# A two-layer encoder on one core: the first layer's entry with all its transfers on one queue, a split second piece and a turn between products

## The reference, cut to what matters

```
h    = rms_norm(x, ev_attn_norm)      # x / sqrt(mean(x*x) + eps) * gain, 256 x 1024
proj = h @ ev_w_in                    # 1024 x 2304
a_q, a_k, a_v, b_q, b_k, b_v = split(proj)
```

## Time and profile before

| | |
|---|---|
| median of 3 runs | 1421.13 us (1420.88 to 1421.44) |
| profiled execution | 1422.96 us, of which span of instructions 1420.8 us |
| PE busy | 1385.0 us, 97% of the span |
| DVE, ACT, POOL busy | 1162.4, 1043.4, 125.9 us |
| moved by DMA | 429.01 MB, mean 302 GB/s |

### The profile page before, as it was taken

One profiled execution on the slowest core, in us unless ns is written; L12 is line 12 of the kernel. 1 busy time (PEld: TensorE's weight loads), 2 busy tenths in 40 slices (PEclk: granted clock), 3 DMA queues, 4 the chain that ended last, 5 costly groups with the idle time before them and its releaser, 6 DMA issues.

```text
span 1420.8 us, 19392 instructions
## 1 busy us (share of the span) xinstructions
PE 1385.0 (97%) x6473; PEld 1133.6 (80%) x6473; DVE 1162.4 (82%) x1450; ACT 1043.4 (73%) x1351; POOL 125.9 (9%) x200
## 2 busy tenths in 40 slices
PE   7999999999899999999999999999999999999997
PEld 5866788888667888888888888888888888888885
DVE  4767555456896999898899989989989998998996
ACT  5566544446785878878878887887888888788786
POOL 0100000000620930000000000000000000000000
PEclk9989999999999999999999999999999999999999
DMA  9603954402807999999999999999999999999980
GB/s 342 257 0 111 363 180 140 144 23 75 326 18 296 371 381 385 376 372 391 363 388 384 369 385 380 380 374 370 393 363 389 388 372 385 370 385 371 373 331 15
DMA packets 132018, 429.01 MB, mean 302 GB/s; under 512 B 4177, under 2 KB 11516, under 8 KB 131980
## 3 DMA queue, kind: packets, MB, share of 16 engines
q1 hardware_dynamic: 126672, 416.82, 77.7%
q0 software_dynamic: 2480, 8.95, 2.5%
q10 hardware_dynamic: 2828, 2.75, 0.6%
HBM read 422.21 MB, written 6.29 MB: 302 GB/s over the span
## 4 chain that ended last, share of the span: by engine, by line
PE 86%; issue 6%; DVE 4%; ACT 2%; DMA 1%; POOL 0%; ACTq 0%; SPq 0%; DVEq 0%; POOLq 0%
PE bank L728 27%; PE bank L730 26%; PE bank L729 26%; PE bank L688 2%; PE bank L865 1%; ACT w_hi L1117 1%; DVE w_lo L1608 1%; DMA xres<-in_x_dram 1%; PE bank L850 0%; PE bank L857 0%; PE bank L849 0%; DMA out_dram<-h,idx_t 0%; PE bank L650 0%; PE bank L923 0%; ACT hT_hi L1145 0%
## 5 line engine op out<-in xcount | busy, mean ns | idle before, releaser
L1536 DVE TENSOR_TENSOR w_lo<-ring,w_hi 128x1024 fp32r<-128x1024 f32 x544 | 644.3, 1220 | 34.8 <-ACT w_hi L1053 20.6
L1053 ACT ACTIVATE w_hi<-ring 128x1024 fp32r<-128x1024 f32 x544 | 571.0, 1062 | 129.7 <-PE bank L730 129.7
L728 PE MATMUL bank<-w_hi,hT_hi 128*128 128x512 f32 (+3 forms) x1088 | 419.2, 385 | 2.4 <-DVE w_lo L1608 1.2
L730 PE MATMUL bank<-w_lo,hT_hi 128*128 128x512 f32 (+3 forms) x1088 | 417.1, 383 | 0.0
L729 PE MATMUL bank<-w_hi,hT_lo 128*128 128x512 f32 (+3 forms) x1088 | 416.9, 383 | 0.0
L728 PEld LDWEIGHTS bank<-w_hi,hT_hi 128*128 128x128 f32 x1088 | 205.1, 189 | 44.4 <-DVE w_lo L1608 3.1
L730 PEld LDWEIGHTS bank<-w_lo,hT_hi 128*128 128x128 f32 x1088 | 205.0, 188 | 40.0
L729 PEld LDWEIGHTS bank<-w_hi,hT_lo 128*128 128x128 f32 x1088 | 205.2, 189 | 39.1
L1608 DVE TENSOR_TENSOR w_lo<-ring,w_hi 128x1024 fp32r<-128x1024 f32 (+3 forms) x124 | 139.5, 1134 | 85.6 <-ACT w_hi L1117 85.4
L728 PE MATMUL bank<-w_hi,aT_hi 128*128 128x512 f32 x490 | 194.8, 398 | 3.4 <-issue 1.9
L730 PE MATMUL bank<-w_lo,aT_hi 128*128 128x512 f32 x490 | 191.6, 391 | 0.0
(11 more groups left out here) (326 smaller groups left out, 1189.7 us busy)
## 6 DMA issues: line engine op xcount, KB each, us to landing
ring<-in_od_e_gate_dram SPq DMA_DIRECT2D x57, 2048.0 KB, 9.5
ring<-in_od_e_up_dram SPq DMA_DIRECT2D x56, 2048.0 KB, 10.3
ring<-in_od_e_down_dram SPq DMA_DIRECT2D x56, 2048.0 KB, 10.1
ring<-in_ev_w_gate_dram SPq DMA_DIRECT2D x5, 2048.0 KB, 8.4
ring<-in_ev_w_up_dram SPq DMA_DIRECT2D x5, 2048.0 KB, 9.7
ring<-in_ev_w_down_dram SPq DMA_DIRECT2D x5, 2048.0 KB, 13.8
ring<-in_ev_w_in_dram SPq DMA_DIRECT2D x3, 2048.0 KB, 22.5
ring<-in_ev_w_out_dram SPq DMA_DIRECT2D x2, 2048.0 KB, 20.5
```

Source lines behind the costliest of these rows:

```text
L728: pe.matmul(dst, hi, whi, start=first, stop=False)
L730: return pe.matmul(dst, hi, wlo, start=False, stop=final)
L1053: act.activation(e_hi_at[place_of(q)], eights(ring[:, i % RING, j * QUARTER:(j + 1) * QUARTER]), ACT.Copy).then_inc(hi_ready, 1)
L1536: dve.tensor_tensor(e_lo_at[place_of(q)], eights(ring[:, i % RING, j * QUARTER:(j + 1) * QUARTER]), e_hi_at[place_of(q)].bitcast(F32), ALU ...
```

## The change

On SP the first constants transfer shrinks to the identity (128 columns instead of 384) and the rest moves behind piece 1. Piece 1 becomes four transfers with a semaphore each. The five transfers of `load_rows` leave ACT's queue for SP's: the bias ones behind piece 1, the sinks and gain rows behind piece 2. PE gets 14 matmuls of 128x128 float32 whose results nobody reads, and turns the second half of x between quarter 0 and quarter 1. ACT and DVE now take stripes 0 and 1 ahead of quarter 0 and stripes 2 and 3 ahead of quarter 1; ACT then does the sums of squares, then quarters 2 and 3, and both take stripes 4 to 7 last. DVE no longer waits for x at the start. The diff, blank lines left out:

```diff
--- before.py
+++ after.py
@@ -284,6 +284,7 @@
         arrived = [sem(f"arrived{i}") for i in range(RING)]
         first_arrived = [sem(f"first_arrived{j}") for j in range(4)]
+        second_arrived = [sem(f"second_arrived{j}") for j in range(3)]
         hi_ready = sem("hi_ready")
         lo_ready = sem("lo_ready")
         quarter_used = sem("quarter_used")
@@ -508,7 +509,19 @@
         @block.sync
         def _(sp):
-            sp.dma_start(cst[:, 0:C_DIST], const[:, 0:C_DIST]).then_inc(consts_loaded, 16)
+            def load_rows(which):
+                if which == "bias":
+                    for dst, keys in ((bias0, P), (bias1, 2 * P)):
+                        src = bass.AP(a["ev_b_rel_bias"].tensor, MAX_REL + 1 - P,
+                                      [[1, P], [2 * MAX_REL + 1, B_HEADS], [1, keys]])
+                        sp.dma_start(dst, src).then_inc(braw_loaded, 16)
+                else:
+                    sp.dma_start(sinks[:, :], a["ev_a_sinks"].to_broadcast([P, A_HEADS])).then_inc(rows_loaded, 16)
+                    sp.dma_start(gq[:, :], a["od_q_norm"].to_broadcast([P, C_QK])).then_inc(rows_loaded, 16)
+                    sp.dma_start(gk[:, :], a["od_k_norm"].to_broadcast([P, C_QK])).then_inc(rows_loaded, 16)
+            sp.dma_start(cst[:, 0:C_TRI], const[:, 0:C_TRI]).then_inc(consts_loaded, 16)
             for half in range(2):
                 cols = slice(half * NW, (half + 1) * NW)
                 sp.dma_start(xres[:, :, cols], x_in[0].rearrange("(t p) d -> p t d", p=P)[:, :, cols])\
@@ -518,8 +531,17 @@
                                  pieces[0]["src"][:, 2 * j:2 * j + 2, :]).then_inc(first_arrived[j], 16)
             for n, p in enumerate(pieces):
                 if n == 0:
-                    sp.dma_start(cst[:, C_DIST:], const[:, C_DIST:]).then_inc(tables_loaded, 16)
                     continue
+                if n == 1:
+                    for j in range(4):
+                        sp.dma_start(ring[:, 1, j * QUARTER:(j + 1) * QUARTER].rearrange("p (k n) -> p k n", k=2),
+                                     p["src"][:, 2 * j:2 * j + 2, :])\
+                          .then_inc(second_arrived[j] if j < 3 else arrived[p["place"]], 16)
+                    sp.dma_start(cst[:, C_TRI:], const[:, C_TRI:]).then_inc(tables_loaded, 16)
+                    load_rows("bias")
+                    continue
+                if n == 3:
+                    load_rows("gains")
                 before = [m for m in range(n) if pieces[m]["place"] == p["place"]]
                 if before:
                     sp.wait_ge(lo_ready, pieces[before[-1]]["q1"])
@@ -945,12 +967,23 @@
                         turn(c if p["kind"] == "up" else c + 1)
+            def idle_matmuls(n):
+                for _ in range(n):
+                    pe.matmul(bank[6][:, 0:P], ones[:, :], ones[:, :], start=True, stop=True)
+            pe.wait_ge(ones_set, 1)
+            idle_matmuls(5)
             pe.wait_ge(consts_loaded, 16)
             pe.wait_ge(gains_loaded, 16)
             pe.transpose(bank[7][:, 0:G_ALL], g_rows[:, :], ident[0:G_ALL, 0:G_ALL]).then_inc(gains_turned, 1)
-            turn_norm(0)
-            for q in range(IN_FIRST):
+            idle_matmuls(3)
+            turn_norm(0, (0, 1))
+            idle_matmuls(6)
+            in_quarter(0)
+            turn_norm(0, (2, 3))
+            for q in range(1, IN_FIRST):
                 in_quarter(q)
             heads0()
             turn_norm(1)
@@ -1108,6 +1141,10 @@
                     p = pieces[n]
                     if n == 0:
                         act.wait_ge(first_arrived[q], 16)
+                    elif n == 1 and q - p["q0"] < 3:
+                        act.wait_ge(second_arrived[q - p["q0"]], 16)
+                    elif n == 1:
+                        act.wait_ge(arrived[p["place"]], 16)
                     elif k0 == 0:
                         act.wait_ge(arrived[p["place"]], 16 * (p["turn"] + 1))
                     if q >= SPLITS:
@@ -1118,36 +1155,9 @@
                        .then_inc(hi_ready, 1)
                     split[0] += 1
-            def load_rows():
-                for dst, keys in ((bias0, P), (bias1, 2 * P)):
-                    src = bass.AP(a["ev_b_rel_bias"].tensor, MAX_REL + 1 - P,
-                                  [[1, P], [2 * MAX_REL + 1, B_HEADS], [1, keys]])
-                    act.dma_start(dst, src).then_inc(braw_loaded, 16)
-                act.dma_start(sinks[:, :], a["ev_a_sinks"].to_broadcast([P, A_HEADS])).then_inc(rows_loaded, 16)
-                act.dma_start(gq[:, :], a["od_q_norm"].to_broadcast([P, C_QK])).then_inc(rows_loaded, 16)
-                act.dma_start(gk[:, :], a["od_k_norm"].to_broadcast([P, C_QK])).then_inc(rows_loaded, 16)
-            def norm(n):
+            def square_sums(n):
                 if n == 0:
-                    act.dma_start(g_rows[:, :], a["gains"]).then_inc(gains_loaded, 16)
-                    act.wait_ge(eps_set, 1)
-                    act.activation(rt[:, 0:1], eps[:, 0:1], ACT.Sqrt)
-                    split_to(1)
-                    act.wait_ge(gain_cols_ready, 1)
-                for k in range(KD):
-                    if n == 0 and k % 2 == 0 and k:
-                        split_to(k // 2 + 1)
-                    if k % 2 == 0:
-                        act.wait_ge(hT_turned, 4 * n + k // 2 + 1)
-                    act.activation(hT_hi[:, k, :], bank[k // 2][:, (k % 2) * SEQ:(k % 2 + 1) * SEQ], ACT.Copy,
-                                   scale=g_cols[:, G_FWD[n] + k:G_FWD[n] + k + 1]).then_inc(hT_hi_ready, 1)
-                if n in SPLIT_FIRST:
-                    split_to(pieces[stage_pieces(SPLIT_FIRST[n])[0]]["q0"] + LEAD)
-                if n == 0:
-                    load_rows()
                     act.wait_ge(x_loaded[0], 16)
                     act.wait_ge(x_loaded[1], 16)
                     act.wait_ge(ones_set, 1)
@@ -1158,6 +1168,29 @@
                 link(sq)
                 act.activation(rt[:, NORM:NORM + TB], ss[:, NORM:NORM + TB], ACT.Sqrt, bias=eps[:, 0:1],
                                scale=1.0 / D).then_inc(norm_sqrt, 1)
+            def norm(n):
+                if n == 0:
+                    act.dma_start(g_rows[:, :], a["gains"]).then_inc(gains_loaded, 16)
+                    act.wait_ge(eps_set, 1)
+                    act.activation(rt[:, 0:1], eps[:, 0:1], ACT.Sqrt)
+                    act.wait_ge(gain_cols_ready, 1)
+                for k in range(KD):
+                    if n == 0 and k == 2:
+                        split_to(1)
+                    if n == 0 and k == 4:
+                        split_to(2)
+                        square_sums(n)
+                        split_to(4)
+                    if k % 2 == 0:
+                        act.wait_ge(hT_turned, 4 * n + k // 2 + 1)
+                    act.activation(hT_hi[:, k, :], bank[k // 2][:, (k % 2) * SEQ:(k % 2 + 1) * SEQ], ACT.Copy,
+                                   scale=g_cols[:, G_FWD[n] + k:G_FWD[n] + k + 1]).then_inc(hT_hi_ready, 1)
+                if n in SPLIT_FIRST:
+                    split_to(pieces[stage_pieces(SPLIT_FIRST[n])[0]]["q0"] + LEAD)
+                if n:
+                    square_sums(n)
             def projection(stage, then=None):
@@ -1881,8 +1915,6 @@
             dve.memset(eps[:, :], EPS).then_inc(eps_set, 1)
             dve.memset(ones[:, :], 1.0).then_inc(ones_set, 1)
-            dve.wait_ge(x_loaded[0], 16)
-            dve.wait_ge(x_loaded[1], 16)
             dve.wait_ge(consts_loaded, 16)
             norm(0)
```

## The result

The changed kernel takes **1416.06 us** in the median of 7 executions (1413.04 to 1417.96), the kernel before 1421.44 us (1418.16 to 1422.76) beside it: ratio 0.9965, 95% interval 0.9955 to 0.9975, so it is faster by about 5 us in 1421, which is small but clear of the interval. The forecast was 1415.8.

The account below looks back on a forecast made before the run. PE bounds the kernel, busy 1385.0 of 1420.8 us, and can still win at the entry: 2.7 + 2.9 + 1.25 - 1.0 - 0.55 = 5.3 us, so the median goes from 1421.13 to 1415.8, range 1413.8 to 1419.6.

Parts of the forecast that it names:

- the first product: On PE at the entry: the first product starts at 10.1 us instead of 12.80, 2.7 us won.
- the 48 products: Quarters 0 to 3 on PE: 48 products in 10.9 instead of 13.84 us at the higher clock, 2.9 us won.
- the wait of 1.25: PE before quarter 4: the wait while ACT issues transfers goes, 1.25 us won.
- the turns: PE between quarters 0 and 1: turning x's second half there costs 1.0 us.
- the new wait: PE before quarter 2: waits for stripes 4 and 5 behind sums of squares and both quarters, 0.55 us lost.
- The 5.3 us that I added to the first unread product: TensorE's clock at the entry: high from about 6.5 us, as 1.1 + 5.3 = 6.4.
- a clock that rises late: Rival at the entry: clock high only at about 13 us, 3.4 us gained, 1417.7; chance 0.15.
- Piece 2: Weights transfer for quarter 8: lands at 29.6 us, 1.6 us before ACT must start at about 31.2.
- the rival: Piece 2 lands 3.6 us later and PE waits 2 us at quarter 8: 1417.8; chance 0.10.
- The heads: Rival in the heads around 80 us: the low-clock stretch falls otherwise, 3 us of either sign, 1419; chance 0.07.
- Slower, at 1427.6: PE between 8.5 and 34 us: unread products don't raise the clock and delay real ones, 6.5 us lost; chance 0.07.

Follow-up runs that it names:

- the kernel with six in the heads: The changed kernel with six more unread products in the heads, four before the sixth head's scores and two before the seventh's: 1413.65 us, ratio 0.9952.

## Why the prediction was right, point by point

**Term by term.** Between the two profiles the first product is 2.3 us earlier (2.7 forecast), the 48 products take 11.4 us instead of 13.84 (2.4 won, 2.9 forecast), the wait of 1.25 is gone, the turns cost 0.8 (1.0) and the new wait 0.37 (0.55): 4.8 us at quarter 4 against the forecast 5.3. The way is the forecast one; that the median, 1416.06, came within 0.3 us of 1415.8 is in part luck, as a median of seven here depends on how many executions kept the clock in the heads.

**The first product**, forecast 10.1, came at 10.49, and for the named reason: with DVE's wait put back it is at 13.85. Two errors of mine nearly cancelled. I had the clock high from 6.5 us, but the first turns still took 1.97 us; only the last unread products show it rising, 12 instructions in 2.41 us where the first ten, at the lower level, took 2.50 and the twelve in the kernel with six in the heads 1.57. The 5.3 us that I added to the first unread product were no fixed time: in the kernel before with only the transfers moved the clock rose 3.5 us after the first product. And x's first half came at 6.18, not 5.87: one queue with less in front of it didn't land it 0.3 earlier. On the other side an unread product costs about 0.5 us at the lower level and 0.26 at the higher one, not 0.59 and 0.33.

**48 products at 0.23 us**: the clock was high from the first on, as forecast, but they gave 2.4 us and not 2.9. Behind every stop (the start, the turns, the wait) the second product follows after 0.30 to 0.33 us and not 0.23, and the 0.37 us in the bracket of the new wait count only from the modelled end of the product before it: from start to start the wait costs 0.55. The case against it, a clock that rises late, costs 1.6 to 1.9 us (the kernels without unread products), near the 1.9 that I gave it (5.3 less 3.4), though I had the unread products slow and in the way there. But the fast products were no term of their own: alone they gave nothing and lost 2.7 us of time (1424.23 against 1421.49 beside it), because the wait for quarter 4 grew to 5.11 us. The sum holds only with all three parts together: each of three undone alone costs 4.9 us (ACT's queue), 4.2 us (DVE's wait) or 1.9 us (unread products) at quarter 4, 11 us together where 4.8 are there to lose. A sum of terms credits each with what the others allow.

**The wait before quarter 4**, 1.25 us: right, and its cause too; the issue on ACT's queue is the cause, shown in both directions. **The turns between products** were costed at 1.0 and the **new wait** at 0.55; measured about 0.8 and 0.37. The turn between products has little worth of its own, 0.1 us, as the sums of squares set quarter 2.

**Piece 2** was forecast at 29.6 us with 1.6 us to spare; it came at 30.9. The sum of bytes took the bias for no slower than other bytes in line; whether the bias is what made it late wasn't tried. PE was still on time by 0.7 us: DVE's part is ready 2.3 us after the transfer (30.94 + 1.05 + 1.2 is 33.2), and quarter 8 starts at 33.96. That margin is no wider than the landing's own spread: with piece 1 as one transfer and with all turns first ACT got piece 2 at 31.52 and 31.81, and quarter 8 came 0.2 us late behind quarter 7. So the rival didn't happen in the changed kernel's profile, but it was near, and piece 2 bounds the next step.

**The heads**: I gave them 3 us of either sign as a rival of 7 in 100. The size was near (2.9 to 4.4 us in the profiles where the clock fell), the kind was wrong. It isn't an effect of the shift alone: the clock stays high in some executions of either kernel and falls in others. How often it falls, read from the mean granted clock, differs (six of seven in the changed kernel, 21 of 28 in the one before, ten of ten with only the transfers moved); whether the kernel or chance sets that isn't shown. And my reading of the median's small range (0.56 us in 3 executions) as the precision of the measurement was mistaken: with 28 the kernel before spans 5.6 us.

**Slower, at 1427.6**, needed a clock that the unread products don't raise. They raised it in each profile that holds them.

## What to carry to other kernels

Measure a change at the entry at the first place where the engines meet again (here quarter 4), and then shut out chance events behind it before asking the total. Ask of a faster engine what it will wait for: products made fast by a warmed clock gained nothing while ACT was held, and the wait took the clock back. The issue of a 4 KB transfer took 7 to 8.5 us on ACT's queue behind 1.5 MB of small rows, and ACT computed nothing for 6.5 to 9.1 us; SP has time for that. Filling a wait with unread products shut out 4 us of chance for some 0.5 us.

## What the runs showed of the hardware

A wait of 1.46 us in a stretch of small products was followed by a fallen clock in eight of ten profiles and not in the other two, and the 28 executions of the kernel before fall into two groups by their mean granted clock (0.995 and more in seven, 0.994 and less in 21). Waits of 3.35, 4.93 and 5.11 us in the entry were followed by slow first products (0.79, 0.79 and 0.80 us), one profile each; waits of 1.25, 1.58 and 2.40 us between or before fast products there were not (0.50, 0.47 and 0.50 us). Four unread products in the 1.46 us wait and two before the next head cost PE some 0.5 us in the profile and took 2.5 us off the median of the kernel before (1421.44 to 1418.92, on one occasion) and 2.4 off that of the changed one (on two). Without unread products the clock rose after 3.9 us of products in one profile (10.04 to 13.91) and only behind quarter 0, 5.3 us, in another, in nearly the same program. What decides between the two wasn't tried.
